# TensorE waits for each half unit singly where units are taken block by block; the mixers' tables are loaded one by one along the feed-forward

## The reference, cut to what matters

```
for l in range(2):
    h = rms_norm(x, ffn1_norm[l]);  x = x + 0.5 * (silu(h @ w_gate) * (h @ w_up)) @ w_down     # 1024 -> 2816 -> 1024
    h = rms_norm(x, mix_norm[l])
    q, k, v of four attentions = split(h @ w_in[l])                                            # 1024 -> 2816
    o = concat(neighbourhood(.., rel_bias), differential(.., lambda), axial GQA, dilated)      # normed with gains
    x = x + o @ w_out[l]
    h = rms_norm(x, ffn2_norm[l]);  x = x + 0.5 * (silu(h @ w_gate) * (h @ w_up)) @ w_down
```

## Time and profile before

| what | value |
|---|---|
| median of 3 runs | 3172.05 us (3170.85 to 3173.61) |
| profiled execution | 3170.26 us |
| its span | 3168.1 us |
| busy: PE / PEld / DVE / ACT / POOL | 95% / 86% / 68% / 51% / 16% |
| mean TensorE clock granted | 0.978 of full |
| DMA | 509.50 MB, mean 161 GB/s |
| weight units on SP's queue | 933 |

### The profile page before, as it was taken

The page is one execution under the profiler, slowest core; times in us unless marked ns, Lnnn a source line. Parts: engine busy times, 40 slices in busy tenths (PEclk is TensorE's granted clock), DMA queues, the critical chain, the costliest instruction groups (busy, mean ns, idle before and its releaser), DMA issues.

```text
span 3168.1 us, 56376 instructions
## 1 busy us (share of the span) xinstructions
PE 3024.1 (95%) x21828; PEld 2725.6 (86%) x21828; DVE 2140.3 (68%) x4498; ACT 1606.6 (51%) x3111; POOL 494.6 (16%) x371
## 2 busy tenths in 40 slices
PE   8989999999998989999999999899989999998999
PEld 8789999978787879999998888799768989976898
DVE  4559988789755456997879955655666556566654
ACT  5445544444555545554444455555545555554554
POOL 1213210000021111330000012132101223210121
PEclk9999999999999999999999999899989999998999
DMA  6345544444554335554444456455414555542354
GB/s 215 120 144 168 182 163 159 161 161 165 188 192 160 137 107 167 167 173 166 156 160 166 161 193 198 167 186 187 133 60 139 188 195 192 186 141 72 127 182 152
DMA packets 138651, 509.50 MB, mean 161 GB/s; under 512 B 15617, under 2 KB 16146, under 8 KB 137106
## 3 DMA queue, kind: packets, MB, share of 16 engines
q1 hardware_dynamic: 134352, 489.22, 46.8%
q10 hardware_dynamic: 4034, 16.69, 1.4%
HBM read 504.80 MB, written 1.05 MB: 160 GB/s over the span
## 4 chain that ended last, share of the span: by engine, by line
PE 84%; DVE 10%; ACT 3%; issue 2%; DMA 1%; POOL 0%; ACTq 0%; DVEq 0%; SPq 0%; POOLq 0%
PE ps L434 83%; DVE WL L1674 2%; ACT WH L1113 1%; PE ps L438 1%; ACT BIG L1222 1%; DMA RAW<-in_w 1%; DVE BIG L1854 1%; DVE XTl L1722 0%; DVE BIG L1759 0%; DVE H L1762 0%; DVE BIG L2138 0%; DVE BIG L2099 0%; DVE BIG L2145 0%; DVE BIG L1737 0%; DVE BIG L1745 0%
## 5 line engine op out<-in xcount | busy, mean ns | idle before, releaser
L1113 ACT ACTIVATE WH<-RAW 128x512 fp32r<-128x512 f32 x1866 | 1157.7, 630 | 1114.0 <-PE ps L434 1095.8
L1674 DVE TENSOR_TENSOR WL<-RAW,WH 128x512 fp32r<-128x512 f32 x1537 | 1112.6, 731 | 751.0 <-ACT WH L1113 738.9
L434 PE MATMUL ps<-XTh,WH 128*128 128x256 f32 x3928 | 1129.6, 288 | 23.0 <-DVE XTl L1901 8.7
L434 PE MATMUL ps<-XTl,WH 128*128 128x256 f32 x3928 | 1118.1, 285 | 0.0
L434 PE MATMUL ps<-XTh,WL 128*128 128x256 f32 x3928 | 1117.5, 284 | 0.0
L2437 POOL TENSOR_TENSOR WL<-RAW,WH 128x512 fp32r<-128x512 f32 x329 | 442.6, 1345 | 2622.8 <-ACT WH L1113 2622.8
L434 PEld LDWEIGHTS ps<-XTh,WH 128*128 128x128 f32 x3928 | 760.2, 194 | 34.0 <-DVE WL L1674 15.3
L434 PEld LDWEIGHTS ps<-XTl,WH 128*128 128x128 f32 x3928 | 761.0, 194 | 3.0
L434 PEld LDWEIGHTS ps<-XTh,WL 128*128 128x128 f32 x3928 | 760.3, 194 | 0.0
L434 PE MATMUL ps<-WH,GH 128*128 128x512 f32 x1056 | 423.6, 401 | 12.1 <-DVE GL L2213 8.1
L434 PE MATMUL ps<-WH,GL 128*128 128x512 f32 x1056 | 416.9, 395 | 0.0
(11 more groups left out here) (192 smaller groups left out, 2614.0 us busy)
## 6 DMA issues: line engine op xcount, KB each, us to landing
RAW<-in_w SPq DMA_DIRECT2D x933, 512.0 KB, 3.3
BIG<-in_ln ACTq DMA_DIRECT2D x4, 1024.0 KB, 6.4
BIG<-in_sk ACTq DMA_DIRECT2D x2, 1024.0 KB, 5.0
BIG<-in_na_bias ACTq DMA_DIRECT2D x2, 1024.0 KB, 7.9
BIG<-in_qk_gain ACTq DMA_DIRECT2D x2, 960.0 KB, 4.9
BIG<-in_memT ACTq DMA_DIRECT2D x4, 256.0 KB, 8.1
BIG<-in_xT ACTq DMA_DIRECT2D x1, 1024.0 KB, 5.5
H<-in_x ACTq DMA_DIRECT2D x1, 1024.0 KB, 8.2
```

The lines of the kernel that those rows point to most:

```text
L434: return self.e.matmul(out, lhsT, rhs, start=start, stop=stop, skip_group_check=loose)
L1113: e.activation(wh, raw, ACT.Copy).then_inc(*c.hi.mark(j))
L1674: e.tensor_tensor(wl, raw, wh.bitcast(F32), ALU.subtract).then_inc(*c.lo_v.mark(j))
```

## The change

`first_rows` and `last_two` take each half by `half` just before its first triple (that of block 0), instead of all four ahead; the wait for the other operand stays at each unit's first half. The order of matmuls is the same.

ScalarE starts the five table loads one at a time: gains at tick 18 of the 132 of the feed-forward, bias at 34, masks and rope at 50, output gain at 62, lambda vectors at 66. GpSimd scales the gains from tick 41 and adds the bias masks from tick 75 on, in the same single steps. The work for lambda leaves the feed-forward: a new generator `lam` runs in the mixer stage, the product and sum on VectorE at its 9th tick, the exponential on ScalarE at its 10th, the difference on VectorE at its 11th. TensorE's `mix_tables` did nothing but count and is gone, as is VectorE's.

```diff
     def first_rows(self, stage, keys, outs):
-        c, held = self.c, []
-        for key in keys[0:2]:
-            for half in range(2):
-                held.append(self.half(key))
-        for blk in range(2):
-            for n, (j, wh, wl) in enumerate(held):
+        c, held = self.c, {}
+        for blk in range(2):
+            for n in range(4):
+                if blk == 0:
+                    held[n] = self.half(keys[n // 2])
+                j, wh, wl = held[n]
                 self.e.wait_ge(*c.xtl.at(stage, *c.chunk(blk, n)))
...
     def last_two(self, stage, units, ready, turn=False):
-        c, held = self.c, []
-        for (key, ah, al), r in zip(units, ready):
-            for half in range(2):
-                held.append((half, ah, al, r, *self.half(key)))
-        for blk in range(2):
-            for n, (half, ah, al, r, j, wh, wl) in enumerate(held):
-                if blk == 0 and half == 0:
-                    self.e.wait_ge(*r)
+        c, held = self.c, {}
+        for blk in range(2):
+            for n in range(4):
+                half, (key, ah, al) = n % 2, units[n // 2]
+                if blk == 0:
+                    if half == 0:
+                        self.e.wait_ge(*ready[n // 2])
+                    held[n] = self.half(key)
+                j, wh, wl = held[n]
...
     # ScalarE
     def mix_tables(self, layer):
-        (five start_load calls)
-        for _ in range(12 + 4 + 8 + 1):
+        loads = {16: ("qkg", t.GAIN, ...), 32: ("nab", t.NABf, ...), 48: ("mc", t.MC, ...), 60: ("dg", t.DG, ...), 64: ("lv", t.LV, ...)}
+        for n in range(65):
+            yield
+            if n in loads:
+                name, dst, src = loads[n]
+                self.start_load(f"{name}{layer}", dst, src)
+
+    def lam(self, layer):
+        for _ in range(9):
             yield
         e.wait_ge(*c.vec.at("lam", layer))
         e.activation(t.lm[:, 2:4], t.lm[:, 0:2], ACT.Exp).then_inc(*c.act.mark("lam", layer))
...
     # ScalarE and VectorE
     def mix_stage(self, layer):
-        pace.fg.append(self.roots(stage))
+        pace.fg += [self.roots(stage), self.lam(layer)]
...
     # VectorE
-    def mix_tables(self, layer):
+    def lam(self, layer):
-        for _ in range(12 + 4 + 8 + 1):
+        for _ in range(8):
             yield
         e.wait_ge(*c.load(f"lv{layer}"))
         e.tensor_tensor(t.lt, t.LV[:, 0:64], t.LV[:, 64:128], ALU.mult).then_inc(*c.vec.mark())
         self.own()
         e.tensor_reduce(t.lm[:, 0:2], t.lt.rearrange("p (a n) -> p a n", a=2), AX, ALU.add).then_inc(*c.vec.mark("lam", layer))
+        yield
+        yield
         e.wait_ge(*c.act.at("lam", layer))
...
     # GpSimd
     def mix_tables(self, layer):
-        for _ in range(12):
+        for _ in range(40):
             yield
         e.wait_ge(*c.load(f"qkg{layer}"))
         (four tensor_scalar, a yield behind each)
+        for _ in range(30):
+            yield
         e.wait_ge(*c.load(f"nab{layer}"))
```

More of the change, by code:

```diff
@@ L956, in peer_stage @@
         self.deepnorm(stage)
-    def mix_tables(self):
-        for _ in range(12 + 4 + 8 + 1):
-            yield
     def ffn_stage(self, layer, which):
         c, stage = self.c, FFN[layer, which]
-        if which == 1:
-            self.pace.fg.append(self.mix_tables())
         self.pace.fg.append(self.roots(stage))
@@ L1518, in mix_tables @@
         c, e, t = self.c, self.e, self.c.mix
[L1519 to L1523, removed]
-        for _ in range(12 + 4 + 8 + 1):
+        loads = {16: ("qkg", t.GAIN, c.small["qk_gain"][layer].unsqueeze(0).to_broadcast([P, 1920])),
+                 32: ("nab", t.NABf, c.small["na_bias"][layer]),
+                 48: ("mc", t.MC, c.small["mix_c"]),
+                 60: ("dg", t.DG, c.small["d_gain"][layer].unsqueeze(0).to_broadcast([P, 64])),
+                 64: ("lv", t.LV, c.small["lam"][layer].unsqueeze(0).to_broadcast([P, 128]))}
+        for n in range(65):
[4 more added lines that the diff above has]
+    def lam(self, layer):
+        c, e, t = self.c, self.e, self.c.mix
+        for _ in range(9):
             yield
@@ L2260, in ffn_stage @@
         stage = FFN[layer, which]
-        if which == 1:
-            self.pace.fg.append(self.mix_tables(layer))
         self.pace.fg.append(self.roots(stage))
```

## The result

The changed kernel takes **3149.52 us** (median of 6 runs), beside 3170.88 us of the kernel before on the same chip: a ratio of 0.9933, 95% interval 0.9919 to 0.9946, or some 21 us less (17.1 to 25.7). One of the six took 9741 us at a granted clock of 0.41 and is not in the ratio; the median of the other five is 3147.69 us. A second set of five runs gave 3145.58 us and 0.9911 (0.9893 to 0.9929, or 22.5 to 33.9 us less). The forecast was 3145 us, 3137 to 3157.

The account below looks back on a forecast made before the run. TensorE, busy 95% of the span, was taken as the bound, with only its holes to win. Terms 5.6 + 0.8 + 8.2 + 2.7 + 5.2 + 4.5 - 0.2 = 26.8 us: 3170.3 to 3143.5, plus 1.8, gives 3145 us; range 3137 to 3157.

Parts of the forecast that it names:

- The five loads: Start of feed-forwards (0,1) and (1,1): delays from the burst of table loads go, 5.6 and 0.8 us.
- the tails: `last_two` in the four feed-forwards: three triples pulled into each hole, 2.1 us each, 8.2 us in all.
- The 0.8 of (1,1): Feed-forward (1,1), also with the burst of loads, is 0.8 us longer than (0,2); this goes.
- The 1.6 twice for slow tails: Tails of feed-forward (0,1) and the last one: half-speed clock behind the hole goes, 1.6 us each.
- The loads one by one: Mid feed-forward: all ten spaced loads cost 0, covered by the stock of four weight units.
- The slower rival: Each large load amid steady weights stops them: 34 us cost, net 3177 to 3179 us; chance 0.03.
- `first_rows`: Two mixer starts: separate waits let triples and block 1 start earlier, 2.6 us each, 5.2 in all.
- `last_two` elsewhere: Tails of GLA, SB and the two mixers: holes of about 0.68 us go, 2.7 us in all.
- PEER, 0: `last_two` in PEER: n = 2 still waits for GL, so 0 gained, twice.
- Lambda in the mixer: VectorE's lambda steps at ticks 9 and 11 of each mixer cost 0.1 us each, 0.2 in all.
- The slow clock: Two feed-forward tails and mixer 5's start: slow clock goes once holes are filled, 1.6 + 1.6 + 1.3 = 4.5 us.
- the rival of the moved clock: Holes in `first_rows` or the deepnorm seams put slow stretches elsewhere: 4.5 us less gained, 3149.5 us; chance 0.2.

Follow-up runs that it names:

- the two parts alone: Kernel before with only the new order of waits: 3148.66 us, 0.9938; kernel before with only the tables and lambda changed: 3170.05 us, 0.9997.
- order-only kernel: Kernel before with the new waits in `first_rows` and `last_two`, tables and lambda as before: 3148.66 us, 0.9938.
- three profiles with those holes: Kernel before (3170.88 us); it with only `first_rows` changed (3165.53 us); it with only tables and lambda changed (3170.05 us).
- the swap: Changed kernel with PEER's last G (127) split between the last two weight halves, on ScalarE and VectorE: 3148.6 us, 0.9929.
- lambda late: Changed kernel with lambda at ticks 19 to 21 of the mixer instead of 9 to 11: 3148.09 us, 0.9932.
- the one without GpSimd at lambda: Changed kernel with one weight half per mixer, split by GpSimd beside lambda's sum, given to VectorE: 3146.43 us, 0.9921.
- swap, lambda in the feed-forward: Changed kernel with PEER's last G split between the last two halves and lambda's work back in the feed-forward: 3150.53 us, 0.9919.
- both PEER swaps with lambda moved: Changed kernel with PEER's last G split earlier, plus lambda in the feed-forward (3150.53 us, 0.9919) or ten ticks later in the mixer (3147.53 us, 0.9922).
- the tables at once: Changed kernel with all five table loads issued together at tick 17 of the feed-forward: 3148.83 us, 0.9932.

## Why the prediction was right, and where not

**The total.** The forecast's sum is 26.8 us. The first set gives 17.1 to 25.7 us, the second 22.5 to 33.9, so the forecast lies just outside the first and inside the second. Of the two parts alone, the order of the waits was forecast at 20.6 us with the clock and measured 14.3 to 25.0; the tables were forecast at 6.2 us and brought no gain that can be told from nothing. So the total lies in the range with one part that shows in it and one that doesn't. By stages the terms can be told apart.

**The five loads** (5.6 and 0.8) **and the tails** (8.2, with 1.6 twice for the clock). Forecast for (0,1) is 5.6 + 2.1 + 1.6 = 9.3 us, measured 9.2; for (1,1) 0.8 + 2.1 = 2.9, measured 2.9; for (0,2) 2.1, measured 2.2; for (1,2) 2.1 + 1.6 = 3.7, measured 3.8. But the first term, "5.6 us, which go", was not one thing. The burst costs 3.4 us with the waits changed (192.3 - 188.9) as with the waits before (194.5 - 191.1), in profiles whose clock stays at 1.00 behind its hole. The other 2.0 us (198.1 - 194.5, less 1.6 for the slow tail) was slow clock in the one profile that I read, behind the hole at 2052; I had taken off only the slow clock of the first matmuls. It is a cost that such a hole may bring, not one that it always brings. (Nor did TensorE stay idle up to 2052.17: it made one transpose at 2051.10 and waited again.) And the hole is not the loads' alone. In the kernel before, a step of `roots` on its chain, with two inputs of 128x1, took 1.10 us at 2049.61 instead of 0.16, beside a split on GpSimd (2049.41, 1.27 us). That stretch is argued from the rows: no run takes GpSimd away there.

The 0.8 of (1,1) is 0.3 by the order-only kernel, so of its 2.9 us some 0.5 stay unexplained. The 1.6 twice for slow tails fits the profile it was read from and no other: in the three profiles with those holes, four of twelve tails were slow, 2.1 us in the mean and not 3.2. That the sums for (0,1) and (1,2) agree to 0.1 us is therefore luck in part: it is the same profile of before that was priced and then compared.

**The loads one by one**, 0: right, and with more cover than I said. I had put the limit near 8 us to land; with a unit at 9.4 us TensorE still runs unbroken, in both feed-forwards. The slower rival is refuted. The Trainium skill (DMA: Bandwidth & Descriptors, Queues, rings and completion order) has each engine take turns between the queues with work, packet by packet. My estimate from it, at most twice the time alone, holds beside a single load (up to 6.8 us in the changed kernel, in (1,1)) and not beside the five: 9.4 us, and 10.3 us at the start of (0,1) in the kernel before, are more than twice 4.0. What makes the difference stays open.

**`first_rows`**, 2.6 each and 1.3 for the clock at mixer 5: 4.4 and 2.9 us, right and a little low.

**`last_two` elsewhere**, 2.7: the waits are gone. Their stages are where the scatter hides them; "rest" came out 1.4 us longer in one profile and 0.6 in the other. In the first PEER of the changed kernel there is one wait of 2.5 us amid the stage (DVE BIG L2161), code that the change doesn't touch; it is 0.7 us in the second profile of the same kernel. PEER, 0: right, and the swap shows that even an unbroken tail there brings nothing that can be measured.

**Lambda in the mixer** is the step that failed. I took 0.1 us each with an upper bound of 0.9, and it measures 1.05 us. The steps were priced by their rows under an idle GpSimd, 0.22 us each, and the bound didn't ask what GpSimd does at tick 9. Where the prediction said "VectorE gets some 0.5 us at tick 9", it got 1.27 us (1.05 + 0.22), and 0.3 us at tick 11, against 0.8 us of room. With the new seam the room was smaller too: with lambda late the scaling of the norm ends at 2245.31, and TensorE turns it at 2245.87 without a wait, 0.56 us later.

```profile
2244.09 1.22 DVE L2324 TENSOR_TENSOR BIG<-BIG 128x1024 f32<-128x1024 f32 x1
```

Lambda's steps without GpSimd would have cost about 0.2 us (above), near the 0.1 forecast; it is the overlap with GpSimd that the term left out.

**The slow clock**, 4.5: right at its three places, wrong as a sum. Slow stretches came elsewhere, which is the rival of the moved clock, and its 3149.5 us is as near to the two sets as the forecast. Mixer 8 by quarters, in the changed kernel and then in the one without GpSimd at lambda (columns as above):

```profile
2785.00:2827.00 42.00, 39.88 (x197) 31.34 (x196) 31.63 (x69) 25.49 (x64) 8.34 (x6) 1.00 0.45 150
2827.00:2869.00 42.00, 39.47 (x196) 30.32 (x194) 30.01 (x67) 20.08 (x55) 3.91 (x3) 0.96 0.27 88
2869.00:2911.00 42.00, 33.69 (x186) 29.37 (x186) 23.89 (x61) 16.12 (x44) 3.04 (x3) 0.80 0.16 51
2911.00:2953.00 42.00, 34.29 (x167) 27.94 (x168) 20.56 (x38) 14.50 (x34) 3.31 (x3) 0.88 0.22 76
```

```profile
2779.00:2819.00 40.00, 38.50 (x189) 30.20 (x189) 30.56 (x67) 25.00 (x64) 6.86 (x5) 1.00 0.44 148
2819.00:2859.00 40.00, 37.60 (x195) 28.98 (x194) 28.46 (x62) 19.50 (x53) 3.90 (x3) 1.00 0.30 102
2859.00:2900.00 41.00, 30.62 (x193) 26.20 (x192) 24.18 (x61) 15.94 (x45) 2.54 (x2) 0.92 0.16 53
2900.00:2940.00 40.00, 32.22 (x168) 26.05 (x167) 22.26 (x43) 15.47 (x37) 3.81 (x3) 0.96 0.23 80
```

The clock falls short by 42 x (0.04 + 0.20 + 0.12) = 15 us in the one and 41 x 0.08 + 40 x 0.04 = 5 us in the other, and the stage takes 167.6 and 161.1 us. Lambda's placing is 0.6 us of this; whether it also tips the clock stays open, as two other versions without the lambda hole took 164.2 us (order only) and 163.5 us (swap, lambda in the feed-forward).

In the last feed-forward, too, four of the later versions (both PEER swaps with lambda moved among them) took 196.2 us where the changed kernel took 194.8, with a slow stretch at its start in code that is the same (granted clock 0.72 from 2948.8 to 2952.8 with the tables at once). These four have no hole at the tails.

So the total was near the forecast by terms that are right by stages (25.4 us in the six columns, forecast 24.5), two of them on slow clock that one profile happened to have, with about 2.1 us of lambda against them, and mixers whose clock scatters by several us.

## What to carry to other kernels

Where an engine takes several buffers and then works through them, let it wait for each one just before its use: the hole shrinks to the last one's lateness, and here nearly all of the gain was that. A burst of side loads was harmless here once the stock of the main stream was full, and cost 3.4 us of a stage when it fell on its start; so move it before you spread it. Before you lay a small VectorE step into a tight chain, look at what GpSimd does in those microseconds, and price a step with two inputs by GpSimd's instruction, not by its own row. Before you price a slow clock from one profile, read a second one.

## What was not expected of the hardware

A VectorE product of 128x64 takes 0.21 to 0.22 us beside an idle GpSimd and 1.05 us beside a GpSimd subtraction of 1.29 us (1.05 or 1.06 us in both mixers of five profiles). Other two-input steps, of 128x1, stretch in the same way, and a one-input step (L1707) doesn't. Timelines of DVE and of POOL in the changed kernel:

```profile
2237.49 0.15 DVE L1707 TENSOR_SCALAR BIG<-BIG 128x1 f32<-128x1 f32 x1
2237.68 1.11 DVE L1709 TENSOR_TENSOR BIG<-BIG 128x1 f32<-128x1 f32 x1
...
2239.47 0.16 DVE L1709 TENSOR_TENSOR BIG<-BIG 128x1 f32<-128x1 f32 x1
...
2237.48 1.29 POOL L2440 TENSOR_TENSOR WL<-RAW,WH 128x512 fp32r<-128x512 f32 x1 [2.99 <-ACT WH L1108]
```

The lost time stands as the VectorE step's own length, not as idle time before it.

Equal holes don't bring equal clocks. The same code with the same two holes in feed-forward (0,1) took 198.1 us in one profile and 194.5 us in another, all of it granted clock; so one profile of before can show a gain of 3.6 us that an edit elsewhere then seems to make.
